# Order of ScalarE's conversions, silus and first product copy at the entry of the feed-forward stages

## The reference

```python
def rms_norm(x, g):
    xf = x.astype(jnp.float32)
    y = xf * lax.rsqrt(jnp.mean(xf * xf, axis=-1, keepdims=True) + RMS_EPS)
    return (y * g.astype(jnp.float32)).astype(x.dtype)

def swiglu(h, w_in, w_out):
    gate, up = jnp.split(h @ w_in, 2, axis=-1)
    return (jax.nn.silu(gate) * up) @ w_out

x = x + 0.5 * swiglu(rms_norm(x, ffn_norm[l, 0]), ffn_w_in[l, 0], ffn_w_out[l, 0])
```

## Time and profile before

| | us |
|---|---|
| median of 3 runs | 2501.09 |
| lowest and highest | 2498.82 to 2501.39 |
| the profiled execution | 2508.27 |
| its span in the trace | 2506.5 |

### The profile page before, as it was taken

How to read it: one execution, slowest core, us unless ns; L and a number is a source line. 1 busy time by engine, 2 the same in 40 slices (tenths; PEclk the granted TensorE clock), 3 DMA queues, 4 the chain that set the end, 5 groups by cost and what they waited for, 6 DMA issues and landing times.

```text
span 2506.5 us, 50199 instructions
## 1 busy us (share of the span) xinstructions
PE 2430.0 (97%) x20010; PEld 2096.0 (84%) x20010; DVE 1499.2 (60%) x2138; ACT 1100.6 (44%) x1959; POOL 719.1 (29%) x357
## 2 busy tenths in 40 slices
PE   8999999998889999999999999999999999999998
PEld 6899887777777889988888889998888777789987
DVE  7987456455763688744432158874453566688743
ACT  4554334634553355533433235553353664445532
POOL 3100443333333410044344440004453101400142
PEclk9999999999997999999999999999999999999999
DMA  4333323210001333333244443333232241333331
GB/s 136 102 101 109 101 80 105 76 47 4 4 4 38 99 101 100 109 101 98 97 150 143 143 132 88 109 109 101 92 107 96 76 136 35 90 96 100 109 101 59
DMA packets 248380, 230.80 MB, mean 92 GB/s; under 512 B 17464, under 2 KB 186584, under 8 KB 248216
## 3 DMA queue, kind: packets, MB, share of 16 engines
q1 hardware_dynamic: 248216, 228.47, 29.3%
HBM read 213.73 MB, written 14.68 MB: 91 GB/s over the span
## 4 chain that ended last, share of the span: by engine, by line
PE 89%; DVE 7%; ACT 2%; issue 2%; POOL 0%; DMA 0%; SPq 0%; ACTq 0%; DVEq 0%
PE bank L377 11%; PE bank L379 10%; PE bank L378 10%; PE bank L906 9%; PE bank L907 9%; PE bank L908 9%; PE bank L384 6%; PE bank L386 6%; PE bank L385 6%; PE bank L2474 1%; PE bank L2461 1%; PE bank L2496 1%; PE bank L1690 1%; DVE hid L779 1%; PE bank L1648 1%
## 5 line engine op out<-in xcount | busy, mean ns | idle before, releaser
L352 POOL TENSOR_TENSOR w_lo<-w_raw,w_hi 128x1024 fp32r<-128x1024 f32 x248 | 614.7, 2486 | 1573.5 <-ACT w_hi L347 1562.3
L347 ACT ACTIVATE w_hi<-w_raw 128x1024 fp32r<-128x1024 f32 x248 | 259.5, 1057 | 518.1 <-PE bank L379 357.4
L687 DVE TENSOR_TENSOR hid_hl<-hid,hid_hl 128x512 fp32r<-128x512 f32 x80 | 186.3, 2332 | 213.1 <-ACT hid_hl L681 213.1
L379 PE MATMUL bank<-hid_hl,w_lo 128*128 128x512 f32 x640 | 249.0, 389 | 0.0
L377 PE MATMUL bank<-hid_hl,w_hi 128*128 128x512 f32 x640 | 249.0, 389 | 0.0
L378 PE MATMUL bank<-hid_hl,w_hi 128*128 128x512 f32 x640 | 249.0, 389 | 0.0
L384 PE MATMUL bank<-w_hi,xg_hi 128*128 128x512 f32 x576 | 226.9, 394 | 0.0
L386 PE MATMUL bank<-w_lo,xg_hi 128*128 128x512 f32 x576 | 224.3, 389 | 0.0
L385 PE MATMUL bank<-w_hi,xg_lo 128*128 128x512 f32 x576 | 224.2, 389 | 0.0
L906 PE MATMUL bank<-xa_hi,w_hi 128*128 128x256 f32 x768 | 218.6, 285 | 0.0
L907 PE MATMUL bank<-xa_lo,w_hi 128*128 128x256 f32 x768 | 218.0, 284 | 0.0
(11 more groups left out here) (349 smaller groups left out, 5872.6 us busy)
## 6 DMA issues: line engine op xcount, KB each, us to landing
w_raw<-in_ffn_w_in SPq DMA_DIRECT2D x352, 256.0 KB, 3.1
w_raw<-in_ffn_w_out SPq DMA_DIRECT2D x176, 256.0 KB, 2.8
w_raw<-in_w_kv SPq DMA_DIRECT2D x96, 256.0 KB, 3.1
w_raw<-in_rwkv_w_rkv SPq DMA_DIRECT2D x48, 256.0 KB, 2.9
w_raw<-in_attn_w_q SPq DMA_DIRECT2D x48, 256.0 KB, 3.1
k_dram<-stage SPq DMA_DIRECT2D x6, 1024.0 KB, 4.6
v_dram<-stage SPq DMA_DIRECT2D x6, 1024.0 KB, 5.5
keys<-k_dram SPq DMA_DIRECT2D x24, 256.0 KB, 3.3
```

Of the source, the lines that this page charges most:

```text
L347: act.activation(w_hi[:, s, :], w_raw[:, s, :], ACT.Copy).then_inc(w_hi_ready, 1)
L352: pool.tensor_tensor(w_lo[:, s, :], w_raw[:, s, :], w_hi[:, s, :].bitcast(F32), ALU.subtract).then_inc(w_lo_ready, 1)
L379: return pe.matmul(o, lo, x_hi, start=False, stop=stop)
L687: dve.tensor_tensor(low, hid_source(k, i), hi.bitcast(F32), ALU.subtract).then_inc(hid_lo_ready, 1)
```

## The change

Only the order of ACT's list is changed, in all four feed-forward stages. The conversion of chunk c0+8 stands ahead of all else that follows c0+7, then come A11 and S1, the conversion of c0+9, and only then the first two silus; S2 and A12, conversion c0+10, and S3, S4 and A22 follow. In tile 0 the first copy stands ahead of weight sums 2 in place of behind it. The third stage's wait for the stores stands behind conversion c0+8, no longer behind c0+9.

```diff
             def frame(n, i=None):
-                his(2 * n + 2, i)
+                if n > 0:
+                    his(2 * n + 2, i)
                 copy(n, P1_DONE, seven_bank(n, C21), seven_bank(n, C11), i)
+                if n == 0:
+                    his(2)
                 if n == 0:
                     for t in range(2 * PLAIN - 2, 2 * PLAIN):
                         silu(t)
...
             for j in range(SLOTS, 2 * SLOTS):
                 split_hi(act, c0 + j)
-            for t in range(2):
-                silu(t)
-            for j in range(2 * SLOTS, 2 * SLOTS + 2):
-                split_hi(act, c0 + j)
+            split_hi(act, c0 + 2 * SLOTS)
             if ph["update"] is None:
                 for i in range(2):
                     act.wait_ge(stored[i], 16 * (len(KV_GROUPS) // 2))
-            normed_his(act, ph, slice(0, 3))
+            normed_his(act, ph, slice(0, 2))
+            split_hi(act, c0 + 2 * SLOTS + 1)
+            for t in range(2):
+                silu(t)
+            normed_his(act, ph, slice(2, 4))
             split_hi(act, c0 + 2 * SLOTS + 2)
-            normed_his(act, ph, slice(3, 7))
+            normed_his(act, ph, slice(4, 7))
             split_hi(act, c0 + 2 * SLOTS + 3)
```

## The result

| | before | after |
|---|---|---|
| median, us | 2499.07 (7 runs) | 2487.48 (7 runs) |
| lowest to highest, us | 2498.50 to 2504.51 | 2482.58 to 2493.27 |
| ratio of the times, 95% interval | | 0.995 (0.9934 to 0.9967) |
| span of the profiled execution, us | 2506.5 | 2481.4 |

The change saves 11.6 us.

A forecast was written before the change was run, and what follows sets the result against it. PE bounds the kernel, losing time in stalls for ACT's copies, late through DVE, and in the slow clock behind them. Gains 11.4 - 1.1 - 2.2 = 8.1; from the median, 2501.1 - 7.6 = 2493.5 us, range 2490 to 2498.

The forecast's parts named there:

- the clock term: Behind P7's stalls in three entries: half a loss of 1.5 us each to the lower clock, 2.2 us in all.
- the lead: DVE's last multiplications before weight sums 2 end 2.6 us earlier; bounds 0.4 and 4.8.
- The rival that the clock stays up: At P7 a stall of 1.75 us never takes the clock down: gain 9.8, 2491.3 us; chance 0.18.
- The median to start from: Time of the kernel before, from which the gain was subtracted: 2501.09 us.
- The entries: First, second and fourth entries into the feed-forward tiles gain 3.5, 3.5 and 4.4 us, together 11.4.
- Tile 1: Its first copy, behind weight sums 4, ends at 101.6 when PE asks at 101.5; 0.2 us allowed.
- The third entry: There DVE is on time and the second copy comes later: a new stall of 1.1 us at P7.
- The fourth entry's longer drop: Its 24 matmuls of P6 and P2 took 0.9 us more in the profiled execution; half was taken off the gain.
- the early subtraction of c0+8: POOL's subtraction moves into DVE's normalisation and costs DVE 2.2 us there.
- The table load: Silu's load on ACT, 1.28 us, now after conversion c0+9, is hidden by 1.4 us.
- the rival that the wait only moves: DVE gains nothing, PE stands 4.35 us at P7 in place of 3.84 at P6: 2503 us; chance 0.14.
- the pause of 2.35 us: DVE's wait for ACT's conversion A11, ahead of A11's remainder; claimed to go in any case.

The follow-up runs named there:

- the second execution: The unchanged change run once more against the kernel before: 2492.89 us (6 runs), ratio 0.9951.
- the pair of 3.13 and 3.14 us: First two stalls at P7 in the change with weight sums 3's conversion repeated twice more ahead of the second copy: 2499.34 us (one run).
- the first half of the change alone: Against the kernel before, only the first copy moved ahead of weight sums 2 in tile 0: 2506.53 us (10 runs), ratio 1.0012.

## Why the prediction was wrong

**The step that failed is the clock term**, 3 x 0.5 x 1.5 = 2.2 us for stalls of 1.75. The stalls were 1.38 to 1.41 (1.35 to 1.40 in the second execution), and these six lost nothing. The size of a loss, 1.5, was right; its chance was not. All fifteen stalls of up to 1.41 us in these runs kept the clock, and the lead, mis-sized by a quarter of a microsecond, put the stalls among them. At the assumed 1.75 half a loss was too much as well, as far as four stalls tell: of those of 1.78 to 1.85 one lost the clock. Over the whole stretch from 1.78 to 3.17 it was a fair price (six of eleven). The rival that the clock stays up, 2491.3 us with a chance of 0.18, was the case that came, though not for its reason that a stall of 1.75 never costs the clock. The Trainium skill (TensorE: Matmul & The Clock Gate, Part 1: The HAM clock gate) adds that the window in which the gate looks at activity runs freely and is not tied to the kernel; by that rule equal stalls can end differently, and the pair of 3.13 and 3.14 us agrees.

This term alone does not explain the miss: without it the forecast is 2491.3, still inside the range, and the time falls below the range only together with the terms that follow. The 6.0 us between forecast and median:

- *Clock*, 2.2, as above.
- *The median to start from*, 2.0. It was 2501.09 over three runs and 2499.07 over seven. The range left no room for that.
- *The entries*, 1.3. The first two tiles gained 3.81, 3.88 and 4.79 where I had 3.5, 3.5 and 4.4. DVE's lead was 2.85, not 2.6, and the second copy came another 0.1 earlier; 0.1 of this was lost again behind P7's stall. Tile 1 gave back 0.15, not 0.2. The third entry lost 0.86, not 1.1.
- *The fourth entry's longer drop*, 0.5, which I had halved. The entries' 11.6 us, with it in full, is what the medians show; with runs that spread over 10 us this part is no finer than their interval.

**What held.** The wait at P6 goes and one at P7 takes its place, by the same ACT line. Each full meeting costs 2.2 us, the early subtraction of c0+8 included: DVE enters the scalings 26.6 us ahead of P1, before 28.8, and the lead comes out by the pause and the count of meetings, as in the prediction's steps from the scalings to the last multiplication. Scalings that read PSUM are not slowed. The table load is hidden: the silus end at 63.63, and DVE wants them at 64.97. That the wait would only move was right for the first half of the change alone, and would have been right for all of it had c0+8 or the silus kept their places.

**What I had too simple.** Against the rival that the wait only moves I set that the pause of 2.35 us goes in any case. The run with c0+8 behind A11 shows that it goes and next to nothing is gained. That c0+8's conversion moves by 10 us was misread: ACT made it at 59.73 before, 11.6 us behind the 48.1 of the prediction. No term hangs on this.

## What to carry to other kernels

Where two engines block each other, count which of their operations meet after the move, not how much earlier each could start: here two silus moved ahead held DVE up by only 0.45 us and yet cost a whole meeting of 2.2, and hiding one more meeting beside work that it doesn't slow won another 4.7 us on top of the 12.5 of the conversions' move. A stall of PE has a price in two parts, its length and then, all or nothing, the clock; where an estimate may fall on either side, give the two as two cases in place of a mean. And when an effect is smaller than the spread of the runs, read it from the stretches that the edit touches, as sums of tile lengths.

## What the runs showed of the hardware

- **The clock after a stall.** Fifteen stalls of 0.83 to 1.41 us all kept it, and twelve of 3.65 to 4.14 all lost it. In between, 1.83, 1.84, 1.85, 2.58 and 3.14 kept it; 1.78, 2.25, 2.27, 2.27, 3.13 and 3.17 lost it. A loss cost 1.5 us in most (15.49 - 3.66 = 11.83 in place of 10.33), and 2.5 in some of the longest (16.97 - 4.13 = 12.84).
- **Which DVE operations POOL blocks.** Those with two operands in SBUF took up to 2.2 us more beside a subtraction of POOL; those with one operand in PSUM took 1.28 as always. The Trainium skill (SBUF — State Buffer, SBUF: two separate sides) describes a port pair that one of the two engines holds for a whole instruction, and counts a DVE operation with two SBUF inputs among those that want it. The rows of these runs agree. The loss does not follow the length of DVE's operation (3.42 for 1.21, 2.62 for 0.42) but what is left of POOL's: with the change POOL's subtractions end at 63.96 and 69.65 and the blocked remainders at 65.04 and 70.74, each 1.1 us later. Where POOL's had begun 1.86 us earlier, the loss was 0.4 (A11's remainder, 1.64 us).
- **A stage that varies by itself.** From the second tile of the first entry to P1 of the second, twelve executions took 779 to 792 us (the change itself 779.09 and 786.29), and the time at the lower granted clock in it was 27 to 58 us, while the stretch from the second entry to the third stayed within 0.1 us. What sets this from one execution to the next was not tried.
